# Routing stage of a gated mixture-of-experts trunk: column-tiled logits, fewer rank products, a one-hot token product for the first job

## The reference, cut to what matters

```python
scores = jax.nn.sigmoid((hf @ w_router).astype(jnp.float32))      # 512 x 16
sel = scores + router_bias.astype(jnp.float32)
grp = sel.reshape(T, N_GROUPS, EXPERTS_PER_GROUP)                 # 4 groups of 4
group_score = lax.top_k(grp, 2)[0].sum(-1)
g_idx = jnp.argmax(group_score, axis=-1)                          # best group
in_grp = jnp.take_along_axis(grp, g_idx[:, None, None], axis=1)[:, 0]
_, loc = lax.top_k(in_grp, TOP_K)                                 # its two best experts
e_idx = g_idx[:, None] * EXPERTS_PER_GROUP + loc
w = jnp.take_along_axis(scores, e_idx, axis=1)
w = w / jnp.sum(w, axis=-1, keepdims=True)
...
for e in range(N_EXPERTS):
    a = jax.nn.silu(hf @ w_gate[e]) * (hf @ w_up[e])
    y = y + comb[:, e:e + 1] * (a @ w_down[e])
```

## Time and profile before

| | |
|---|---|
| median of 3 executions | 938.93 us (937.58 to 940.26) |
| profiled execution | 940.68 us, its span 938.8 us |
| PE, share of the span busy | 90% |
| PE weight loads (PEld) | 66% |
| DVE | 51% |
| ACT | 22% |
| POOL | 22% |
| mean granted PE clock | 0.951 of full speed |
| memory traffic | 182.81 MB read, 10.49 MB written |

### The profile page before, as it was taken

One profiled execution on the slowest core, in us unless ns is written; L12 is line 12 of the kernel. 1 busy time (PEld: TensorE's weight loads), 2 busy tenths in 40 slices (PEclk: granted clock), 3 DMA queues, 4 the chain that ended last, 5 costly groups with the idle time before them and its releaser, 6 DMA issues.

```text
span 938.8 us, 13350 instructions
## 1 busy us (share of the span) xinstructions
PE 843.6 (90%) x5250; PEld 621.9 (66%) x5250; DVE 480.8 (51%) x604; ACT 202.0 (22%) x260; POOL 209.7 (22%) x217
## 2 busy tenths in 40 slices
PE   2799999999999999979999998479999979999970
PEld 0478899988799877768777697445555535555530
DVE  3543887896579966768999364501111101111116
ACT  4331211213331135512222333100000000000012
POOL 0000402121722200523444140012222212222220
PEclk9899999999999999999999899679999989999995
DMA  9913131212121211176675929849599999799416
GB/s 317 346 46 117 62 126 36 65 46 90 45 91 46 73 63 45 46 269 228 220 230 179 370 81 366 343 149 394 195 395 391 394 398 400 302 388 354 163 35 268
DMA packets 102392, 191.80 MB, mean 204 GB/s; under 512 B 4275, under 2 KB 41411, under 8 KB 102349
## 3 DMA queue, kind: packets, MB, share of 16 engines
q1 hardware_dynamic: 89150, 160.79, 47.3%
q10 hardware_dynamic: 9168, 19.40, 6.0%
q0 software_dynamic: 4032, 11.03, 3.3%
HBM read 182.81 MB, written 10.49 MB: 206 GB/s over the span
## 4 chain that ended last, share of the span: by engine, by line
PE 74%; DVE 10%; DMA 5%; SPq 4%; issue 4%; ACT 2%; POOL 0%; DVEq 0%; POOLq 0%; ACTq 0%
PE proj L823 16%; PE proj L550 12%; PE proj L552 11%; PE proj L551 11%; PE ha L859 8%; PE pp L643 5%; DVE ada_acc L1399 3%; SPq L442 3%; DMA w_raw<-in_w_in 2%; PE pp L813 1%; DMA ew<-in_w_gate 1%; PE ha L710 1%; DMA ada_p<-in_w_ada 1%; SPq L461 1%; PE pp L629 1%
## 5 line engine op out<-in xcount | busy, mean ns | idle before, releaser
L823 PE MATMUL proj<-ew,heT 128*64 128x256 f32 x1536 | 179.8, 388 | 7.3 <-DMA ew<-in_w_gate 4.1
L823 PEld LDWEIGHTS proj<-ew,heT 128*64 128x64 f32 x1536 | 109.8, 140 | 76.3 <-issue 20.3
L550 PE MATMUL proj<-h_hi,w_hi 128*128 128x512 f32 x368 | 147.8, 402 | 9.3 <-DVE h_lo L1182 7.8
L552 PE MATMUL proj<-h_hi,w_lo 128*128 128x512 f32 x368 | 144.5, 393 | 0.0
L551 PE MATMUL proj<-h_lo,w_hi 128*128 128x512 f32 x368 | 144.3, 392 | 0.0
L1695 POOL TENSOR_TENSOR w_lo<-w_raw,w_hi 128x2048 fp32r<-128x2048 f32 x15 | 71.1, 4740 | 103.0 <-ACT w_hi L905 103.0
L859 PE MATMUL ha<-ew,aT 128*64 128x512 f32 x384 | 87.9, 599 | 1.5 <-DVE aT L1630 0.9
L550 PEld LDWEIGHTS proj<-h_hi,w_hi 128*128 128x128 f32 x368 | 69.8, 190 | 28.7 <-issue 14.4
L1303 DVE SCALAR_TENSOR_TENSOR acc<-u_t,cols_t,acc 128x512 f32<-128x512 f32 x120 | 85.8, 775 | 0.0
L905 ACT ACTIVATE w_hi<-w_raw 128x2048 fp32r<-128x2048 f32 x36 | 68.7, 1909 | 78.7 <-PE proj L552 52.4
L552 PEld LDWEIGHTS proj<-h_hi,w_lo 128*128 128x128 f32 x368 | 69.7, 189 | 15.0
(11 more groups left out here) (233 smaller groups left out, 1301.3 us busy)
## 6 DMA issues: line engine op xcount, KB each, us to landing
ew<-in_w_gate SPq DMA_DIRECT2D x32, 1024.0 KB
ew<-in_w_up SPq DMA_DIRECT2D x32, 1024.0 KB, 15.0
ew<-in_w_down SPq DMA_DIRECT2D x32, 1024.0 KB, 15.1
w_raw<-in_w_in SPq DMA_DIRECT2D x28, 1024.0 KB, 5.0
ada_p<-in_w_ada ACTq DMA_DIRECT2D x16, 1024.0 KB, 5.4
ada_w<-in_w_ada SPq DMA_DIRECT2D x8, 1024.0 KB, 13.3
w_raw<-in_w_o_hgrn SPq DMA_DIRECT2D x4, 1024.0 KB, 5.0
w_raw<-in_w_out SPq DMA_DIRECT2D x4, 1024.0 KB, 7.4
```

The costliest lines, as they stand in the source:

```text
L550: pe.matmul(outap, a_hi, b_hi, start=first, stop=False)
L552: return pe.matmul(outap, a_lo, b_hi, start=False, stop=last)
L823: mm = pe.matmul(out_ps[JS * i:JS * i + JS, 0:FG], heT[:, c_, JS * j_:JS * j_ + JS], w[:, k, FG * i:FG * i + FG], start=(kb == 0), stop=(k ...
```

## The change

1. **Logits in column tiles.** The eight feature blocks of a tile are spread over four column tiles of the array: the stationary operand is 32 wide (two routers' blocks side by side; only one of them is used), block 4h+j goes to PSUM partitions 32j to 32j+31. Four partial sums, for j = 0 to 3, result. DVE copies them to `lgt` (128x128 per tile), and a product with a constant 128x16 selector `sel` adds the four and turns the result to tokens by experts. ACT takes the sigmoid of 128x64 after that, straight into rt[0]; a PSUM copy on DVE goes.
2. **Ranks.** Eight products (one, six and one) become three; DVE first sums `chosen` over tiles with three additions of 16 columns, a copy and another addition. DVE reads ranks and counts from PSUM where it copied or reduced them before.
3. **Tokens of job 0.** DVE makes `place0`, the one-hot of expert 0's ranks 0 to 63, and PE multiplies h2 (in SBUF, not transposed) with it: 32 products, stationary 128x128, moving 128x64, straight into the layout that ACT copies to `heT`. The gather of job 0 and its four transposes go; the gather of job 1 is the first, and all later counts shift by one.
4. **One-hot steps.** `slot1` is made by one operation 64 wide per choice instead of eight operations 128 wide; the token number goes into `job1` by an added multiplication. The index product is issued for both halves of the partitions from a 64-wide stationary operand: 16 products for eight.
5. **Weights of the experts' outputs** (`wsel`) are worked out after the job table and not while the ranks run; a memset moves ahead of the choice. ACT waits for h2's writes to DRAM (s_h2w) before it overwrites h2 with the first `heT`.

```diff
@@ logits, on PE
             def logits(tt):
                 pe.wait_ge(s_h2c, tt + 1)
-                for k in range(KT):
-                    mm = pe.matmul(pp[0:NE, P * tt:P * tt + P], cols_t[:, C_WR + NE * k:C_WR + NE * k + NE],
-                                   h2T[:, k, P * tt:P * tt + P], start=(k == 0), stop=(k == KT - 1))
-                return mm
+                if tt == 3:
+                    pe.wait_ge(s_lc, 1)
+                for h in range(2):
+                    for j in range(4):
+                        kb = 4 * h + j
+                        c0 = C_WR + NE * (kb if j < 3 else kb - 1)
+                        mm = pe.matmul(logit_ps[tt][32 * j:32 * j + 32, :], cols_t[:, c0:c0 + 32],
+                                       h2T[:, kb, P * tt:P * tt + P], start=(h == 0), stop=(h == 1))
+                mm.then_inc(s_lg, 1)
...
-            pe.wait_ge(s_sc, 1)
+            pe.wait_ge(s_sl, 3)
             for tt in range(TT):
-                mm = pe.transpose(pp[:, 512 + NE * tt:512 + NE * tt + NE], sc_T[:, P * tt:P * tt + P], ident[0:NE, 0:NE])
+                pe.wait_ge(s_lc, tt + 1)
+                mm = pe.matmul(pp[:, 512 + NE * tt:512 + NE * tt + NE], lgt[:, P * tt:P * tt + P], sel[:, 2, :],
+                               start=True, stop=True)
             mm.then_inc(s_sT, 1)
 
             pe.wait_ge(s_dv, 1)
-            chosen = rt[:, 20, :]
-            pe.matmul(pp[:, 576:640], tri, chosen, start=True, stop=False)
-            for t2 in range(TT - 1):
-                for tt in range(t2 + 1, TT):
-                    pe.matmul(pp[:, 576 + NE * tt:576 + NE * tt + NE], ones, chosen[:, NE * t2:NE * t2 + NE],
-                              start=False, stop=(t2 == TT - 2))
-            pe.matmul(pp[:, 640:704], ones, chosen, start=True, stop=True).then_inc(s_rk, 1)
-
-            pe.wait_ge(s_oh1, 2 * TT)
+            pe.matmul(pp[:, 576:640], tri, rt[:, 20, :], start=True, stop=False)
+            pe.wait_ge(s_cu, 2)
+            pe.matmul(pp[:, 592:640], ones, rt[:, 25, 0:48], start=False, stop=True)
+            pe.matmul(pp[:, 640:656], ones, rt[:, 25, 48:64], start=True, stop=True).then_inc(s_rk, 1)
+
+            pe.wait_ge(s_p1, 1)
+            for kb in range(KT):
+                q = P * (kb % (KT // GT)) + JS * (kb // (KT // GT))
+                for tt in range(TT):
+                    mm = pe.matmul(pp[:, q:q + JS], h2_t[:, tt, P * kb:P * kb + P], place0[:, tt, :],
+                                   start=(tt == 0), stop=(tt == TT - 1))
+            mm.then_inc(s_xp, 1)
+
+            pe.wait_ge(s_oh1, 1)
             pe.wait_ge(s_oj, 1)
             for c in range(2 * TT):
-                mm = pe.matmul(pp[:, 704:704 + NPOS], slot1[:, c, :], job1[:, c, :], start=(c == 0), stop=(c == 2 * TT - 1))
+                for i in range(GT):
+                    mm = pe.matmul(pp[JS * i:JS * i + JS, 704:704 + NPOS], slot1[:, c, :], job1[:, c, :],
+                                   start=(c == 0), stop=(c == 2 * TT - 1))
             mm.then_inc(s_ix, 1)
...
-            tokens(0, True)
@@ on ACT
-            act.wait_ge(s_lg, 1)
-            act.activation(sc_T[:, :], pp[0:NE, 0:T], ACT.Sigmoid).then_inc(s_sc, 1)
+            act.wait_ge(s_sT, 1)
+            act.activation(rt[:, 0, :], pp[:, 512:576], ACT.Sigmoid).then_inc(s_sc, 1)
...
+            act.wait_ge(s_h2w, 16 * TT)
             tokens_out(0, True)
@@ on DVE, after the choice (the block of wsel stands behind job_table_done now)
+            tt_(r(25, 16, 32), chosen[:, 0:16], chosen[:, 16:32], ALU.add)
+            tt_(r(26, 0, 16), chosen[:, 32:48], chosen[:, 48:64], ALU.add)
+            go(dve.tensor_copy(r(25, 0, 16), chosen[:, 0:16]))
+            settle()
+            dve.tensor_tensor(r(25, 32, 48), r(25, 16, 32), chosen[:, 32:48], ALU.add).then_inc(s_cu, 1)
+            dve.tensor_tensor(r(25, 48, 64), r(25, 16, 32), r(26, 0, 16), ALU.add).then_inc(s_cu, 1)
...
+            go(dve.scalar_tensor_tensor(col(key), by_tt(chosen)[:, :, 0:1], -1024.0, by_tt(rank)[:, :, 0:1], ALU.mult, ALU.add))
+            settle()
+            dve.scalar_tensor_tensor(place0[:, :, :], io[:, 0:JS].rearrange("p (o s) -> p o s", o=1).broadcast_to([P, TT, JS]),
+                                     -1024.0, col(key).broadcast_to([P, TT, JS]), ALU.add, ALU.is_equal).then_inc(s_p1, 1)
...
-            for c in range(2 * TT):
-                dve.tensor_scalar(slot1[:, c, :].rearrange("p (g s) -> p g s", g=GT),
-                                  io[:, 0:JS].rearrange("p (o s) -> p o s", o=1).broadcast_to([P, GT, JS]),
-                                  r(18, c, c + 1), con_t[:, K_VAL + c:K_VAL + c + 1],
-                                  ALU.is_equal, ALU.mult).then_inc(s_oh1, 1)
+            dve.tensor_tensor(slot1[:, :, :], io[:, 0:JS].rearrange("p (o s) -> p o s", o=1).broadcast_to([P, 2 * TT, JS]),
+                              col(r(18, 0, 8)).broadcast_to([P, 2 * TT, JS]), ALU.is_equal).then_inc(s_oh1, 1)
...
-            dve.memset(nst[:, 0:1], 0.0).then_inc(s_oj, 1)
+            dve.tensor_tensor(job1[:, :, :], job1[:, :, :], col(con_t[:, K_VAL:K_VAL + 2 * TT]).broadcast_to([P, 2 * TT, NPOS]),
+                              ALU.mult).then_inc(s_oj, 1)
```

More of the change, by code:

```diff
@@ L216, in trunk_kernel @@
         rt = at("rt", "ON0", [P, 32, TT * NE])
-        slot1 = at("slot1", "ON0", [P, 2 * TT, P], F32, 8192)
+        slot1 = at("slot1", "ON0", [P, 2 * TT, JS], F32, 8192)
+        place0 = at("place0", "ON0", [P, TT, JS], F32, 8192 + 8 * TT * JS)
         job1 = at("job1", "MASK", [P, 2 * TT, NPOS])
@@ L1463, in _ @@
             w4 = con_t[:, K_W4:K_W4 + 4].rearrange("p (o e) -> p o e", o=1)
+            for tt in range(TT):
+                dve.wait_ge(s_lg, tt + 1)
+                dve.tensor_copy(lgt[:, P * tt:P * tt + P], logit_ps[tt]).then_inc(s_lc, 1)
+            go(dve.memset(r(19, 0, 16), 0.0))
             dve.wait_ge(s_ys, 16)
-            dve.wait_ge(s_sT, 1)
-            scores = pp[:, 512:512 + TT * NE]
-            tt_(by_tt(r(1)), by_tt(scores), rb_t[:, :].rearrange("p (o e) -> p o e", o=1).broadcast_to([P, TT, NE]), ALU.add)
-            go(dve.tensor_copy(r(0), scores))
+            dve.wait_ge(s_sc, 1)
+            tt_(by_tt(r(1)), by_tt(r(0)), rb_t[:, :].rearrange("p (o e) -> p o e", o=1).broadcast_to([P, TT, NE]), ALU.add)
             settle()
@@ L1511, in _ @@
             dve.tensor_tensor(r(20), r(13), r(14), ALU.add).then_inc(s_dv, 1)
-            both = rt[:, 13:15, :].rearrange("p c (a e) -> p (c a) e", e=NE)
             twice = lambda ap: ap.rearrange("p (o n) -> p o n", o=1).broadcast_to([P, 2, TT * NE])
-            tt_(rt[:, 15:17, :], twice(r(0)), rt[:, 13:15, :], ALU.mult)
-            go(dve.memset(r(19, 0, 16), 0.0))
-            settle()
-            go(dve.tensor_reduce(wsel[:, :, :].rearrange("p a b -> p (a b)"),
-                                 rt[:, 15:17, :].rearrange("p c (a e) -> p (c a) e", e=NE), AX.X, ALU.add))
@@ L1528, in _ @@
+            go(dve.tensor_copy(r(25, 0, 16), chosen[:, 0:16]))
+            settle()
+            dve.tensor_tensor(r(25, 32, 48), r(25, 16, 32), chosen[:, 32:48], ALU.add).then_inc(s_cu, 1)
+            dve.tensor_tensor(r(25, 48, 64), r(25, 16, 32), r(26, 0, 16), ALU.add).then_inc(s_cu, 1)
             dve.wait_ge(s_pt, GT)
             dve.wait_ge(s_rk, 1)
-            rank, div, slot, job = r(21), r(22), r(23), r(24)
-            cnt, nb, incl, start = [r(17, 16 * a, 16 * a + 16) for a in range(4)]
@@ L1532, in _ @@
-            go(dve.tensor_reduce(cnt, pp[:, 640:704].rearrange("p (a e) -> p e a", a=TT), AX.X, ALU.add))
-            go(dve.tensor_copy(rank, pp[:, 576:640]))
+            rank, cnt = pp[:, 576:640], pp[:, 640:656]
+            div, slot, job = r(22), r(23), r(24)
+            nb, incl, start = [r(17, 16 * a, 16 * a + 16) for a in range(1, 4)]
+            io = con_t[:, K_IO:K_IO + P]
+            key = r(21, 0, TT)
+            go(dve.scalar_tensor_tensor(col(key), by_tt(chosen)[:, :, 0:1], -1024.0, by_tt(rank)[:, :, 0:1], ALU.mult, ALU.add))
@@ L1602, in _ @@
             dve.memset(nst[:, 1:2], 0.0).then_inc(s_jb, 1)
+            tt_(rt[:, 15:17, :], twice(r(0)), rt[:, 13:15, :], ALU.mult)
+            settle()
+            go(dve.tensor_reduce(wsel[:, :, :].rearrange("p a b -> p (a b)"),
+                                 rt[:, 15:17, :].rearrange("p c (a e) -> p (c a) e", e=NE), AX.X, ALU.add))
+            settle()
+            tt_(r(18, 16, 20), wsel[:, 0, :], wsel[:, 1, :], ALU.add)
+            settle()
+            go(dve.reciprocal(r(18, 20, 24), r(18, 16, 20)))
+            settle()
+            tt_(wsel[:, 0, :], wsel[:, 0, :], r(18, 20, 24), ALU.mult)
+            tt_(wsel[:, 1, :], wsel[:, 1, :], r(18, 20, 24), ALU.mult)
             dve.wait_ge(s_ix, 1)
```

52 lines of the change are left out of this document (26 added, 26 removed).

## The result

The changed kernel took 930.56 us, the median of 4 executions (928.81 to 933.25); the kernel before, beside it, 939.6 (937.58 to 944.34). The ratio is 0.9912 with a 95% interval of 0.9888 to 0.9935: 0.9% faster, where 931.7 us were predicted. The gain between the medians is 9.0 us, where I had 7.2. The profiled execution took 930.0 us, its span 928.2.

What follows compares the result with a forecast made beforehand. It took PE, mostly idle or slow in a serial stage before the first expert product, as the bound. Earlier logits (3.7 us), shorter ranks (1.9) and a token product replacing the gather gave 7.2 us less: 931.7 us, range 927.5 to 938.5.

Steps and rivals of the forecast that it cites:

- Step A: Logits up to the choice: column tiles run side by side, gain 3.7 us, bounds 0 and 4.7.
- Step B: Rank products after the choice: 6 rows for 16, gain 1.9 us, bounds 1.5 and 2.4.
- Step C: Token product after the ranks: 64 rows at the low clock throughout, 13.9 us, bounds 7.3 and 13.9.
- the sum: First transposes to first gate product: the gate product begins at 611.4 for 618.65, 7.2 us less.
- Step D: Index product: 64-wide rows run in pairs, 1.9 us, bounds 1.0 and 6.8; DVE's shorter `slot1` hidden beside the token product.
- Step E: Behind the index product: index arithmetic and gather, now job 1's, leave the path; with transposes and copy they took 7.1 us.
- The rest moves rigidly: From the gate product on: it starts at the low clock as before, so the 7.2 us carry through to the end.
- 1, the clock rises in the token product: Token product: unbroken work raises the clock 4.3 us in, 7.2 us more gained, 924.5 us; chance 0.13.
- 2, the gain shrinks: Logits keep the low clock or index rows don't pair: 2.6 or 4.9 us lost, 934.3 to 936.6; chance 0.13.
- my 1.1: Logits: the gain in us if the clock stays low through the whole stage, instead of 3.7.
- 3, the weight stream stays: Expert loop: the wait for weights near 760 is tied to time and grows by the gain, 938.9 us; chance 0.05.
- 4, tiled rows one after the other: Logits and index product: column-tiled rows run serially, 10.2 us lost of 7.2, 941.9 us; chance 0.05.

Runs made afterwards that it cites:

- both together: The change with the token product turned over (one-hot stationary, h2 streaming 512 wide) plus ten unused wide rows ahead of the choice; 921.73 us, timed again 920.62 us.
- the filled kernel: The change plus ten wide rows of unused work on PE while it waits for the choice; 928.71 us, ratio 0.9889.

## Why the prediction was right

**Step A, logits: right in kind, taken too small.** The price was 3.7; in like conditions it is 4.4 to 4.8. With the low clock in the first logits of both (the change, twice, against the logits undone and against the second profile of before) the rank products start 4.4 to 4.75 us sooner, at my upper bound of 4.7. With the high clock there in both it is the same: the second profile of both together, whose code is the change's up to the choice, has

```profile
578.03 3.34 PE L776 MATMUL ha<-con_t,h_t 128*128 128x128 f32 x16 [4.52 <-DVE h_t L1465]
581.30 0.64 PE L788 MATMUL proj<-h2T,cols_t 128*32 128x128 f32 x16
...
585.68 0.64 PE L788 MATMUL proj<-h2T,cols_t 128*32 128x128 f32 x16 [0.54 <-ACT h2T L1088]
...
592.11 0.43 PE L810 MATMUL pp<-rt,con_t 128*128 128x64 f32 x2 [0.41 <-DVE rt L1545]
```

and the rank products come at +14.08, for +18.56 in the earlier trace rows: 4.5. Only between the first two profiles was it 3.2 (+15.38 for +18.56), because the change's profile had the low clock in its first logits and the other had not; that stretch costs 1.1 to 1.3 us in either kernel. Two terms were mis-sized. The last logits end 8.3 us after the first transpose here, where I had 8.7. And from there to the rank products it takes 5.8 us in both kernels (596.93 - 591.18 and 593.04 - 587.26), where I had 0.3 more for the change. Rows in four column tiles do run side by side. The change of tiling costs little: from the start of a tile's logits to the start of the next transposes it is 584.42 - 583.84 = 0.58 us, 0.12 more than the 0.46 of the rows' price, and the eight transposes behind take 1.02 from start to start, as before. So the Trainium skill's rule (TensorEngine Tiling, Key Properties) that a change of mode drains the engine has a price of about 0.1 us here, not that of a whole row.

**Step B, ranks: right.** 1.9 predicted, 1.9 by undoing it.

**Step C, tokens: the size is right, its worth was not said.** 13.9 us predicted at the low clock, 13.91 measured, and 27.57 for twice the rows. What the sum hid is that this product gained nothing: with the gather put back the gate product comes 0.4 to 0.6 us sooner. The gain of the whole change is A, B and the index rows (4.5 + 1.9 + 1.5 = 7.9 in like conditions, 6.8 to 8.1 between the profiles), less that half a us.

**Step D, index product: right.** 1.9 predicted, 1.92 measured; 3.57 from 128-wide weights. That `slot1` is free was right as well, through the token product's cover: `job` is ready 8.4 us early. Where the cover is gone (gather put back), PE waits 5.86 us for it and `slot1`'s saving would count.

**Step E and the sum: right, with a part missing.** 33.1 us from first transpose to gate product predicted, 33.45 and 33.23 measured. That it is so close is in part luck: A was 0.8 us too small, and the low clock in the change's first logits, which the sum does not have, cost 1.1 to 1.3. "The rest moves rigidly" failed by 3 us in the good direction, through the clock behind the wait for weights. The time came out 1.1 us under the forecast and not 3; the four executions of the change scatter by 4.4 us, so this agreement is no test of the last us either.

**Rivals.** 1, the clock rises in the token product: refuted. The Trainium skill (TensorE: Matmul & The Clock Gate, "Why this matters for your kernels") asks for a TensorE busy without a break; here 27.57 us without a break left the clock at 0.50, while a wide product raised it on the way. The trace does not bear out the rule for products of this shape. 2, the gain shrinks: no, the index rows pair, and a low clock in the first logits leaves A as it is; my 1.1 reckoned with the new rows' price at that clock and not with what the old ones cost at it. No profile had the low clock through the whole stage of logits. 3, the weight stream stays: no; SP waits 21.6 us for 22.6, and PE's wait for weights became shorter, not longer. 4, tiled rows one after the other: no, 0.65 us for a tile.

**One sentence of the argument bears more than its row showed.** I wrote that 64-column products kept a high clock. The row at 201.58 there has 64-wide weights, but the stretch at clock 1.00 holds products of the token product's own shape (timeline of PE, kernel before):

```profile
147.85 3.68 PE L643 MATMUL pp<-q_t,k_t 128*128 128x64 f32 x32
```

They stand in a longer run of work without a gap and kept 1.00 to their end. In the filled kernel rows of this shape were at 1.00 for only 1.6 us, behind short rows and waits. So the sentence holds for what it says, and the fall in the filled kernel is not explained by the shape of the rows alone; whether the short rows and waits ahead did it was not tried. The other row that I leaned on is weaker too: the 32 one-column products (L629) took 4.71 us and lost the clock there, but with the logits undone and with the token product twice over the same products took 3.63 us and the clock stayed at 1.00.

## What to carry to other kernels

Filling an idle engine is not a gain by itself: ask what the chain that it replaces takes, and put that chain back as an experiment. When the stationary operand is wide and the moving one narrow, the time here was the loading of weights (busy 9.00 of 9.00 us). Try the product turned over, so that the one-hot is stationary and the data stream 512 wide, even at the price of a copy and four transposes: the gate product came 6.9 us sooner. And before reading a difference of a few us between two profiles, profile each kernel twice and compare from a common event, since the code ahead of it moves by itself.

## What the runs showed of the hardware

- Rows of 64 columns under 128-wide float32 weights come every 0.215 us at 1.2 GHz and left the clock there for 27.57 us. Behind short rows and waits it fell 1.6 us into them in one profile; behind unbroken work 32 of them kept 2.4 GHz for 3.68 us. Rows of 512 columns in two column halves raised it: 0.50 in the first 4.7 us, 1.00 after.
- Rows with 64-wide weights in different column halves run in pairs: 32 rows in 1.92 us, 16 rows 128 wide in 3.57, both at 1.2 GHz. At 2.4 GHz a pair takes 0.95 / 16 = 0.059 us (602.32 to 603.27 with the product turned over), no more than one such row by itself, 2.08 / 32 = 0.065.
- Sixteen rows of 128 columns take 0.65 us in four column tiles and 1.92 us without (2.4 GHz).
- The gather of 64 rows takes as long with the memory busy as nearly idle: from POOL's first copy for it to PE's transposes 4.36 us with the gather put back (602.30 to 606.66, 295 GB/s) and 4.37 before (612.48 to 616.85, 51 GB/s).
- The same work ahead of the stage ended up to 6 us apart between profiles (574.32 to 580.37). The latest has stretches of 1.2 GHz near 54 and 140 us that the earliest lacks.
